# Gates of a product-key expert layer: indirect accumulating DMAs in place of one-hot matmuls

## The reference, cut to what matters

```
q = h2 @ wq; scores = q . keys              # per token, head (8) and half (2): 128 scores
s_top, i_top = top_k(scores, 16)            # both halves
best, pos = top_k(s_top[0] + s_top[1], 16)  # 16 of 256 pairs -> expert = i0 * 128 + i1
gates = softmax(best)
act = gelu(u[expert] . h2); out = sum(gates * act * v[expert])
```

## Time and profile before

| | us |
|---|---|
| median of 3 runs | 1760.81 (1755.99 to 1762.16) |
| profiled execution, its own time | 1756.99 |
| its span, first to last instruction | 1755.3 |
| busy: TensorE, VectorE, ScalarE, GpSimd | 1598.4, 1218.9, 660.7, 506.8 |
| granted TensorE clock, mean | 0.967 |

### The profile page before, as it was taken

The page is one execution under the profiler, slowest core; times in us unless marked ns, Lnnn a source line. Parts: engine busy times, 40 slices in busy tenths (PEclk is TensorE's granted clock), DMA queues, the critical chain, the costliest instruction groups (busy, mean ns, idle before and its releaser), DMA issues.

```text
span 1755.3 us, 26062 instructions
## 1 busy us (share of the span) xinstructions
PE 1598.4 (91%) x7931; PEld 1352.1 (77%) x7931; DVE 1218.9 (69%) x2080; ACT 660.7 (38%) x1039; POOL 506.8 (29%) x612
## 2 busy tenths in 40 slices
PE   8999889899898998888987798866999999999998
PEld 4877445369887898878987688866888888888886
DVE  4403523118999877998779967756887878888885
ACT  2103445114433365433563246622333333333332
POOL 4542002000042311223211221244653433444340
PEclk9899789999999999999998999998999999999999
DMA  5222040011497755998558895599999999999995
GB/s 205 72 72 92 6 156 1 0 60 49 122 297 226 232 192 176 293 303 270 179 187 241 255 322 186 187 371 331 371 396 339 342 335 344 352 361 353 354 349 207
DMA packets 187082, 402.98 MB, mean 230 GB/s; under 512 B 16272, under 2 KB 114576, under 8 KB 186512
## 3 DMA queue, kind: packets, MB, share of 16 engines
q1 hardware_dynamic: 150160, 268.02, 44.9%
q0 software_dynamic: 36864, 134.23, 21.8%
HBM read 347.67 MB, written 54.53 MB: 229 GB/s over the span
## 4 chain that ended last, share of the span: by engine, by line
PE 35%; DVE 25%; issue 7%; ACT 6%; DMA 2%; SPq 1%; ACTq 1%; DVEq 1%; POOL 0%; POOLq 0%
PE psum L972 30%; DVE ulo L1534 5%; PE psum L534 5%; DVE urow L1539 4%; DVE hotB L1645 3%; ACT uhi L1212 2%; ACT hotB L1239 2%; SPq L359 1%; DVE cand L1610 1%; DVE cand L1613 1%; ACT stage L1248 1%; DVE routed L1616 1%; DMA urow<-in_u,idx 1%; DVE h2row L1539 1%; DVE itop L1579 1%
## 5 line engine op out<-in xcount | busy, mean ns | idle before, releaser
L534 PE MATMUL psum<-hhi,uhi 128*128 128x384 f32 x1024 | 358.9, 351 | 37.6 <-ACT uhi L1212 37.6
L534 PE MATMUL psum<-hlo,uhi 128*128 128x384 f32 x1024 | 352.6, 344 | 0.0
L1309 ACT ACTIVATE vhi<-vraw 128x1024 fp32r<-128x1024 f32 x128 | 136.0, 1062 | 305.1 <-PE psum L972 298.7
L534 PE MATMUL psum<-hhi,ulo 128*128 128x384 f32 x1024 | 207.1, 344 | 44.8 <-DVE ulo L1534 44.5
L1534 DVE TENSOR_TENSOR ulo<-h2T,uhi 128x1024 fp32r<-128x1024 f32 x128 | 156.8, 1225 | 122.6 <-ACT uhi L1212 117.0
L972 PE MATMUL psum<-vhi,wlo 128*128 128x512 f32 x768 | 236.5, 389 | 0.0
L972 PE MATMUL psum<-vlo,whi 128*128 128x512 f32 x768 | 236.4, 389 | 0.0
L972 PE MATMUL psum<-vhi,whi 128*128 128x512 f32 x768 | 236.4, 389 | 0.0
L534 PEld LDWEIGHTS psum<-hhi,uhi 128*128 128x128 f32 x1024 | 201.1, 196 | 42.6 <-ACT uhi L1212 42.5
L534 PEld LDWEIGHTS psum<-hhi,ulo 128*128 128x128 f32 x1024 | 179.9, 190 | 57.9 <-DVE ulo L1534 57.7
L516 POOL DMA_INDIRECT urow<-in_u,idx x96 | 106.9, 1113 | 391.9 <-DVE urow L1539 377.1
(11 more groups left out here) (258 smaller groups left out, 2269.6 us busy)
## 6 DMA issues: line engine op xcount, KB each, us to landing
h2T<-in_uT SPq DMA_DIRECT2D x128, 512.0 KB
vraw<-in_v SPq DMA_DIRECT2D x128, 512.0 KB
acts_scratch<-act_s SPq DMA_DIRECT2D x128, 192.0 KB
gring<-gates_scratch SPq DMA_DIRECT2D x128, 192.0 KB
aring<-acts_scratch SPq DMA_DIRECT2D x128, 192.0 KB
gates_scratch<-wring SPq DMA_DIRECT2D x24, 512.0 KB
gates_scratch<-stage SPq DMA_DIRECT2D x24, 512.0 KB
wring<-in_chunks SPq DMA_DIRECT2D x23, 512.0 KB, 4.0
```

The lines of the kernel that those rows point to most:

```text
L534: return nc.tensor.matmul(out, lhsT, rhs, start=start, stop=stop)
L1309: a_(vhi[:, k, :], vraw[:, k, :], ACT.Copy).then_inc(s["vhi_ready"], 1)
```

## The change

- `gates_d` is zeroed: GpSimd clears a strip `zeros` (in `yg`), and SyncE stores it 128 times over in each of eight DMAs, put among the trunk's chunk loads (`ZERO_AT`, after chunks 8, 10 ... 22). VectorE waits for them before `yg` is used.
- The one-hots, `turned`, `weigh`, `gates`, `stage_gates` and `store_gates` are gone. `route(t)` now leaves, for each of the 128 (head, k) columns, an address in `gates_d` per token (`sidx`) and the gate (`sgate`). GpSimd issues for each tile and column one indirect DMA that adds 128 single elements into memory (`add_gates`). The columns of one head have different experts; heads may share one, so before head h it waits until head h - 1 has landed (`added`). SyncE waits for all of `added` before it loads gates.
- Gathers are written out with no loop, read their indices from `eidx` itself, and have eight buffers (`urow` in `wring`). They stand in GpSimd's program between the heads of the adds: 22 before the first add, 14 beside tile 1's adds, 14 beside tile 2's, 4 per head beside tile 3's, the rest after.
- `uhi` and `ulo` have four buffers, ScalarE rounds two blocks ahead (`AHEAD`), `sco` has two and `wf` has two instead of four. The routes now carry 8, 28, 28 and 28 split blocks (`LOWERED`) and 0, 16, 14 and 14 dots (`DOTTED`); the 84 dots that remain are spread over the 32 blocks after them. `LAST_U` moves slightly.

```diff
-R = [(0, 2), (2, 8), (12, 17), (21, 25)]
-H = [(8, 12), (17, 21), (25, 29)]
+R_SCORES = [0, 2, 9, None]
+UR = 8
+LOWERED = [8, 28, 28, 28]
+DOTTED = [0, 16, 14, 14]
+AHEAD = 2
+LAST_U = [0, 4, 8, 14, 20, PASSES]
+ZERO_AT = list(range(RING, RING + 16, 2))
...
+                if n in ZERO_AT:
+                    rows = NK * P // (P * len(ZERO_AT))
+                    sp.dma_start(gates_d.rearrange("(p i) j t -> p (i j) t", p=P)[:, rows * ZERO_AT.index(n):rows * (ZERO_AT.index(n) + 1), :],
+                                 zeros.unsqueeze(1).broadcast_to([P, rows, TD])).then_inc(s["gates_zero"], 16)
...
+            def gather(table, n, used, at):
+                k = n % UR
+                if n >= UR:
+                    pool.wait_ge(row_in[k], 16 * (n // UR))
+                    pool.wait_ge(s[used], at)
+                g.indirect_dma_start(urow[k], None, table, bass.IndirectOffsetOnAxis(eidx[:, n % HK:n % HK + 1], 0)).then_inc(row_in[k], 16)
...
+            def add_gates(tt, h):
+                if h:
+                    pool.wait_ge(added[tt][(h - 1) % 2], 16 * TOPK * ((h - 1) // 2 + 1))
+                for k in range(TOPK * h, TOPK * (h + 1)):
+                    g.indirect_dma_start(flat, bass.IndirectOffsetOnAxis(sidx[:, tt, k:k + 1], 0), sgate[:, tt, k:k + 1], None,
+                                         compute_op=ALU.add).then_inc(added[tt][h % 2], 16)
             pool.wait_ge(s["eidx_ready"], 1)
+            pool.wait_ge(s["gates_zero"], 16 * len(ZERO_AT))
+            gather_u(UR + DOTTED[1] - 2)
+            for t in range(1, NT):
+                pool.wait_ge(s["routed_ready"], t + 1)
+                n = gathered[0]
+                for h in range(PH):
+                    add_gates(t - 1, h)
+                    if t < NT - 1:
+                        gather_u(n + DOTTED[t + 1] * (h + 1) // PH)
+                    else:
+                        gather_u(n + 4 * (h + 1))
+            gather_u(HK)
...
-            for t in range(1, NT):
+            for t in range(NT):
                 route(t)
-                hot(t - 1)
...
+            while lowered[0] < NK - 4:
+                left = NK - 4 - lowered[0]
+                up_to(lowered[0] + 1, dotted[0] + -(-(HK - dotted[0]) // left))
```

More of the change, by code:

```diff
@@ L279, in trunk @@
         act_stored = [sem(f"act_stored{i}") for i in range(4)]
-        row_in = [sem(f"row_in{i}") for i in range(4)]
+        row_in = [sem(f"row_in{i}") for i in range(UR)]
+        added = [[sem(f"added{t}_{e}") for e in range(2)] for t in range(DT)]
         def bank(name):
@@ L353, in store_act, with pass_u @@
                 sp.dma_start(acts_d[i], act_s[:, k, :]).then_inc(act_stored[k], 16)
[L355 to L362, removed]
+            def pass_u(q):
                 for k in range(4):
[L364 to L367, removed]
                     if not (isinstance(q, int) and q == PASSES - 1):
@@ L384, in _ @@
             pass_u(0)
-            with sp.Fori(1, H[0][1]) as q:
+            a = (sum(LOWERED) + 8) // 4
+            with sp.Fori(1, a) as q:
                 pass_u(q)
-            for tt in range(DT):
[L389 to L412, removed]
+            sp.wait_ge(s["routed_ready"], NT)
+            for k in range(4):
+                load_v(k, k)
+            with sp.Fori(a, PASSES - 2) as q:
+                pass_u(q)
+            pass_u(PASSES - 2)
+            for tt in range(DT):
+                for e in range(2):
+                    sp.wait_ge(added[tt][e], 16 * HK // 2)
             for k in range(4):
@@ L902, in ups @@
                         up(k, 4 * q + k)
[L904 to L915, removed]
+            pe.sem_inc(s["p1_done"], 4)
             key_scores(0)
@@ L934, in _ @@
             pe.wait_ge(s["pq_ready"], PH + 2)
[L935 to L955, removed]
-            pe.wait_ge(s["g_free"], 16 * DT + 2)
+            a = 0
+            for t in range(1, NT):
+                ups(a, R_SCORES[t - 1])
+                key_scores(t)
+                a = R_SCORES[t - 1]
+            ups(a, PASSES - 1)
+            pe.wait_ge(s["sco_ready"], 4 * NT)
             pe.wait_ge(s["zero_ready"], 1)
@@ L1214, in activations @@
-            def activations(k, q):
-                before = (k - 1) % 4
-                act.wait_ge(s["p1_done"], 4 * q + (k + 2))
-                act.wait_ge(act_stored[before], 16 * q + (16 if k else 0))
-                a_(act_s[:, before, :], psum[:, before % 2, 0:TD], ACT.Gelu).then_inc(s["act_ready"], 1)
-            def tile(k, q):
-                upper_u(k, q)
-                if not (isinstance(q, int) and q == 0 and k == 0):
-                    activations(k, q)
-            def tiles(a, b):
-                if a == b:
-                    return
-                with act.Fori(a, b) as q:
-                    for k in range(4):
-                        tile(k, q)
@@ L1668, in _ @@
[L1668 to L1669 removed]
+                else:
+                    link(v.tensor_scalar(sidx[:, t - 1], routed[:, 0, :], float(TD), rowid[:, t - 1:t], ALU.mult, ALU.add))
+                dve.sem_inc(s["routed_ready"], 1)
+                up_to(sum(LOWERED[:t + 1]), sum(DOTTED[:t + 1]))
+            for t in range(NT):
                 route(t)
[L1671 removed]
             v.memset(zr[:].bitcast(F32), 0.0).then_inc(s["zero_ready"], 1)
[L1673 removed]
```

307 lines of the change are left out of this document (100 added, 207 removed).

## The result

The changed kernel takes 2114.62 us (median of five runs, 2105.35 to 2354.92), the kernel before beside it 1760.81: ratio 1.1999, 95% interval 1.1969 to 1.2029. One of the five, 2354.92, ran at a granted clock of 0.69 (0.86 in the others) and stands outside the ratio. A second set of runs of the same kernel gave 2107.86 us and a ratio of 1.1972 (1.1925 to 1.2019). The forecast was 1737 us; the time lies 378 above it, and above the range's 1905. The expectation for that set weighed two theories: about 2113 us if each add keeps GpSimd busy whatever the other engines do, under 1850 if the low clock had made the kernel slow. The first held.

A forecast was written before the change was run, and what follows sets the result against it. Only the upward phase could give, with GpSimd's adds as the new chain: first add 590, adds done 1081, downward at 1190 instead of 1213.5, 24 us less, so 1737 us forecast; range 1660 to 1905.

The forecast's parts named there:

- term (2): Upward phase, GpSimd: 384 indirect adds priced from gathers, 1.09 us each in the routes and 0.97 in the tail.
- rival A: GpSimd: adds cost more than gathers, 0.43 us each, 165 us for 384, making 1902 us in all; chance 0.28.
- Zeros: Trunk: eight stores of 3.1 MB among the chunk loads cost 0, or 20 us if the ring's lead were used up.
- First add: Upward phase, GpSimd: the first add goes out at about 590 us, after 107 us of VectorE work.
- Waits between heads: GpSimd: each head's 16 adds must land before the next head's, 26 us of waiting, 90 from above.
- rival B: Landing between heads: 4-byte pieces are slow in the DMA engines; at 6.3 us landing, 1801 us in all; chance 0.15.
- Last stretch: After the adds, from 1081: 100 us for 46 rows and 19 blocks, then 9 us to the first downward product.
- Downward: Last phase, 128 blocks on TensorE: starts at 1190, not 1213.5, and again lasts 541 us.
- Routes 2 and 3: Upward phase: 121 us each by TensorE, ending at 711 and 832, well before their adds can begin.
- Rival D: GpSimd: adds so cheap, say 0.6 us, that it is no bound; downward at 1024, 1571 us in all; chance 0.10.
- Rival E: Downward phase: deeper rings hide nothing, since it has no gap; already in the sum, no chance given.

The follow-up runs named there:

- the mixture: The kernel before, with tile 1's gates made by adds, tiles 2 and 3 by one-hots, one written-out gather after every second add: 1732.94 us, ratio 0.982.

## Why the prediction was wrong

**The step that failed is term (2), the price of the adds**, taken from the durations of the earlier trace rows: 1.09 us each in the routes and 0.97 in the tail. Measured, an add is 1.71 us busy on average and 0.30 more to the next instruction. From the first add to the end of the last I had 491 us (403 of adds, 62 of 60 gathers, 26 of waits) and the chip took 846. The parts, from the profile after (GpSimd is busy 711.3 us from the first add to the end of the last, 656.3 in adds and 55.0 in 56 gathers):

```profile
593.90:1440.20 846.30, 343.70 (x1726) 335.56 (x1725) 262.49 (x617) 113.18 (x152) 711.32 (x440) 0.70 0.48 97
```

| | forecast | measured | difference |
|---|---|---|---|
| 384 adds, busy | 403 | 656 | +253 |
| gathers beside them (60, 56) | 62 | 55 | -7 |
| 0.30 us in front of each of 440 | 0 | 132 | +132 |
| waits for landings between heads | 26 | 2.5 | -24 |

The parts come to 354 of the 355 us of difference. Of the 253, accumulating is 384 x (1.556 - 0.972) = 224, shown by the store in its place. The rest, 29, is that standing behind VectorE was undersized: a mean of 1.709 over a median of 1.556 makes 59 us on 384 adds, where I had 30. That part is read from the spread of the durations; no run has it by itself. The mechanism itself held; at 599.60 an add met VectorE's dot, which has two SBUF inputs, and took 2.37:

```profile
598.18 1.23 DVE L1442 TENSOR_TENSOR ulo<-h2T,uhi 128x1024 fp32r<-128x1024 f32 x1
599.32 1.22 DVE L1448 SCALAR_TENSOR_TENSOR wring<-wring,h2row 128x1024 f32<-128x1024 f32 x1
599.60 2.37 POOL L517 DMA_INDIRECT gates_scratch<-sgate,sidx  x1 [0.30 <-issue]
```

The dot ends at 600.54 and the add 1.43 us later; the gather of the earlier trace rows ended 0.84 after VectorE did, and the 0.59 between them is about what accumulating costs.

The two failures differ in kind. That accumulating costs more was rival A, at 0.28, and no row of before could price it; I gave it 0.43 us where it is 0.58, and the range left out "an add at twice a gather's price", and from start to start that is nearly what came (1.86 against 0.97). The gap stood in the rows: the earlier trace rows has it in brackets, 0.29 us between the copy of an index and its gather, and I took the duration beside it. As the program of before waits there for the copy, the rows could not tell whether the gap would go with the copies, but I left it out without asking. The run with written-out gathers has it with no copy:

```profile
487.83 0.94 POOL L511 DMA_INDIRECT urow<-in_u,eidx  x1 [0.30 <-issue]
```

It costs 132 us; with it alone in the sum the forecast would have been about 1870, on the other side of 1761. For an engine that works without a pause, the price is the interval between two starts.

**What held, and what was off without deciding.** *Zeros* at 0: the trunk ends at 401.75. *First add* near 590: 593.9. *Waits between heads*: 26 us were forecast, 2.5 came; an add lands in 3.1 us (median), mostly within the gathers between heads, and rival B falls for this kernel. (With more traffic beside them, in the mixture with two gathers per three adds, adds land in 4.9 us at the median and 128 of them wait 13.6 us.) The Trainium skill, "DMA: Bandwidth & Descriptors", Specifications, has transfers below 512 B done as read-modify-write, short of line rate; no wait of this kernel shows such a loss. Its "GPSIMD Engine Reference", section 8, names contention with VectorE instructions that have two SBUF inputs, and the profile after agrees: 2.37 us for 1.556 at 599.60, behind such a dot. *Last stretch*: 109 forecast, 120 measured, at 390 GB/s. *Downward*: 541.8 forecast as before, 543.5. Start + 4, adds + 355, last stretch + 11 give the 370 us by which downward starts later than 1190.

*Routes 2 and 3* were to end at 711 and 832. They end at 781 and 1059 (710 and 827 without adds): their blocks and dots waited for gathers that stood behind the adds. That cost this kernel little, as GpSimd set the end, but it is the second price of the adds, and I had it only for the time after 832. It follows from the first: as an estimate, 16 adds and 1.75 gathers at 1.09 us and a wait of 1.6 bring 1.75 rows in 21 us, which with six rows in hand makes about 26 of the 28 that the two routes need by 832; at the measured price they come in about 35 us. *Rival D's* floor, 1571 us with downward at 1024, is what the kernel without adds showed: 1564.47 and 1011. *Rival E* held in its part: deeper rings win nothing in downward. My expectation of one tile's adds failed by the same oversight. The 33 to 53 us from more gathers beside the last tile failed by another: on a full engine order moves work, and doesn't remove it.

What stays open: why accumulating costs GpSimd 0.59 us more, and what the 0.30 us between two indirect DMAs is. The runs show their sizes, not their causes.

## What to carry to other kernels

Price an instruction of an engine that will run without a pause by the interval between two starts, not by its duration, and where a new kind of DMA is the whole case, measure one before building on it. An engine that issues in program order makes everything behind a batch late: put what other engines wait for first, at the rate at which they use it, and let the work with slack fill in; in the mixture one condition in the loop was worth 41 us. A change that loses as a whole can win in part: one tile of three made by adds, in that order, is 4% faster than the kernel before.

## What the hardware showed

- An indirect DMA that accumulates holds GpSimd 1.556 us, one that only stores 0.970, a gather of 4 bytes 0.944 and one of 4 KB rows 0.972. Adding at 64 places in place of 128 saves 0.146 us. (All medians.)
- Between two indirect DMAs of GpSimd lie 0.30 us that no wait explains, the same for adds, stores and gathers (115 us on 384).
- Adds of 128 single elements land in 3.1 us (stores 2.2), and heads almost never had to wait: 2.5 us in all. At a DMA share of 0.87 (0.44 to 0.57 here) they landed in 4.9 us.
- An add issued 0.28 us into a VectorE operation with two SBUF inputs took 2.37 us, not 1.556.
- TensorE's granted clock was 0.83, 0.68 and 0.60 on average in the three stretches of adds, the last two mostly at its 1.2 GHz level (0.5), while it worked 185 of 279, 98 of 273 and 61 of 285 us. There GpSimd set the pace. In the last stretch the clock was 0.90 and in downward, where TensorE sets it, 0.99.
